# Attention scores in float32 high and low parts: from six matmuls over 64 rows to four over 128 rows

## The reference

```python
z = jnp.einsum("bqhd,bkhd->bhqk", qb, kb).astype(jnp.float32) * scale
strict = s_pos < t_pos
log_keep = jnp.where(strict, jax.nn.log_sigmoid(-z), 0.0)
after = lax.cumsum(log_keep, axis=3, reverse=True) - log_keep
weights = jnp.where(strict, jnp.exp(jax.nn.log_sigmoid(z) + after), 0.0)
outs.append(jnp.einsum("bhqk,bkhd->bqhd", weights.astype(v.dtype), vb))
```

## Time and profile before

| | us |
|---|---|
| median of 3 runs | 2956.75 (2955.31 to 2957.13) |
| the profiled execution's own time | 2955.53 |
| its span, first to last instruction | 2953.8 |
| PE busy | 2770.1 (94% of the span) |
| DVE busy | 1511.2 (51%) |
| ACT busy | 1077.0 (36%) |
| POOL busy | 985.1 (33%) |
| mean granted TensorE clock | 0.967 of full speed |
| attention stage, first score matmul to the last product | 1573.64 to about 2543 |

### The profile page before, as it was taken

One profiled execution on the slowest core, in us unless ns is written; L12 is line 12 of the kernel. 1 busy time (PEld: TensorE's weight loads), 2 busy tenths in 40 slices (PEclk: granted clock), 3 DMA queues, 4 the chain that ended last, 5 costly groups with the idle time before them and its releaser, 6 DMA issues. The chain is left out here.

```text
span 2953.8 us, 40091 instructions
## 1 busy us (share of the span) xinstructions
PE 2770.1 (94%) x14914; PEld 2031.1 (69%) x14914; DVE 1511.2 (51%) x1689; ACT 1077.0 (36%) x1590; POOL 985.1 (33%) x694
## 2 busy tenths in 40 slices
PE   4999999999999989979997999999999999689998
PEld 3999999888888857756664555555555555368887
DVE  6112445210000010008996888888889888565554
ACT  4010101111111131101114778777778777432221
POOL 1211121121211200007775655656566556200000
PEclk6999999999999999989997999999999999889999
DMA  3232221323212211114444122121221210342331
GB/s 117 85 116 99 79 71 64 114 107 118 74 64 71 78 58 67 45 45 120 129 128 140 58 58 73 37 87 51 58 87 35 82 30 26 117 137 87 98 99 43
DMA packets 165312, 239.96 MB, mean 81 GB/s; under 512 B 11152, under 2 KB 117904, under 8 KB 157504
## 3 DMA queue, kind: packets, MB, share of 16 engines
q1 hardware_dynamic: 163456, 238.25, 25.2%
q10 hardware_dynamic: 1728, 0.03, 0.0%
HBM read 141.49 MB, written 96.76 MB: 81 GB/s over the span
## 5 line engine op out<-in xcount | busy, mean ns | idle before, releaser
L1399 POOL TENSOR_TENSOR a_w<-a_beta,a_rest 128x1024 f32<-128x1024 f32 (+2 forms) x320 | 560.3, 1751 | 341.3 <-DVE a_rest L1351 311.8
L352 PE MATMUL f_acc<-ut_hi,f_w_hi 128*128 128x512 f32 (+2 forms) x1568 | 582.4, 371 | 14.6 <-POOL f_w_lo L337 14.6
L352 PE MATMUL f_acc<-ut_lo,f_w_hi 128*128 128x512 f32 (+2 forms) x1568 | 584.6, 373 | 0.0
L352 PE MATMUL f_acc<-ut_hi,f_w_lo 128*128 128x512 f32 (+2 forms) x1568 | 583.2, 372 | 0.0
L1351 DVE TENSOR_TENSOR_SCAN a_rest<-a_keep,a_rest,a_ones 128x513 f32<-128x513 f32 x384 | 466.8, 1262 | 11.0 <-ACT a_keep L1321 11.0
L1270 PE MATMUL a_turn<-a_ident,a_w 128*128 128x128 f32 (+1 forms) x2432 | 352.7, 280 | 28.1 <-DVE a_wt L1304 26.0
L1270 PEld LDWEIGHTS a_turn<-a_ident,a_w 128*128 128x128 f32 (+1 forms) x2432 | 257.4, 140 | 123.1 <-issue 64.9
L334 POOL TENSOR_TENSOR f_w_hi<-f_stage,f_zero 128x1024 fp32r<-128x1024 f32 x44 | 83.3, 1893 | 770.7 <-DMA f_stage<-in_w_blocks 770.7
L1285 PE MATMUL a_o<-a_wt,a_v 128*64 128x512 f32 (+3 forms) x1408 | 338.5, 559 | 0.0
L352 PEld LDWEIGHTS f_acc<-ut_hi,f_w_hi 128*128 128x128 f32 x1568 | 295.1, 188 | 51.0 <-issue 15.3
L352 PEld LDWEIGHTS f_acc<-ut_lo,f_w_hi 128*128 128x128 f32 x1568 | 295.0, 188 | 34.7
(11 more groups left out here) (172 smaller groups left out, 3415.8 us busy)
## 6 DMA issues: line engine op xcount, KB each, us to landing
f_stage<-in_w_blocks SPq DMA_DIRECT2D x44, 512.0 KB, 5.5
scratch_gate<-f_row_a SPq DMA_DIRECT2D x16, 1024.0 KB, 4.6
o_g<-scratch_mixed SPq DMA_DIRECT2D x32, 512.0 KB, 5.4
scratch_xbc<-f_row_a SPq DMA_DIRECT2D x12, 1032.0 KB, 4.8
s_xc<-scratch_xbc SPq DMA_DIRECT2D x16, 768.0 KB, 5.3
scratch_k_hi<-f_row_a SPq DMA_DIRECT2D x8, 1032.0 KB, 3.9
scratch_k_lo<-f_row_b SPq DMA_DIRECT2D x8, 1032.0 KB, 6.9
n_xin<-in_x SPq DMA_DIRECT2D x16, 512.0 KB, 3.5
```

The costliest lines, as they stand in the source:

```text
L352: last = nc.tensor.matmul(acc[c][:, 0:tn], w[s][:, k, :], u[:, k, t0:t0 + tn], start=(k == 0 and u is ut_hi and w is w_hi), stop=(k == KB ...
L1399: nc.gpsimd.tensor_tensor(w[r % AS][:, :, 0:tn], beta[r % KEEPS][:, :, 0:tn], rest[r % RS][:, :, 1:tn + 1], ALU.mult).then_inc(w_ready, 1)
```

## The change

The queries of a unit are no longer two tiles but one, `q`, whose rows 0 to 63 hold the high part and rows 64 to 127 the low part of one head, the head being a second dimension. The keys' high and low tiles get the same second dimension, with a head's 64 channels written twice, on rows 0 to 63 and again on rows 64 to 127. One matmul over 128 rows then gives q high times k plus q low times k; with k high and k low that is two matmuls for a head, four for a unit, each over the full array height. The product of the two low parts, which was left out before, is now in the sum. The mask matmul of a head follows its two products. Who copies what (`on_act`) is as before.

```diff
-        k_high, k_low = ring("k_high", 2, (P, T), F32R), ring("k_low", 2, (P, T), F32R)
+        k_high, k_low = ring("k_high", 2, (P, 2, T), F32R), ring("k_low", 2, (P, 2, T), F32R)
-        q_high, q_low = ring("q_high", 2, (P, W), F32R), ring("q_low", 2, (P, W), F32R)
+        q = ring("q", 2, (P, 2, W), F32R)
...
                 for tile, name in ((k_high, "k_hi"), (k_low, "k_lo")):
-                    sp.dma_start(tile[slot][:, t0:t1].bitcast(F32),
-                                 scratch[name][pair, :, t0:t1]).then_inc(k_loaded[slot][part], 16)
+                    for half in range(2):
+                        sp.dma_start(tile[slot][half * HEAD:(half + 1) * HEAD, :, t0:t1].bitcast(F32),
+                                     scratch[name][pair, :, t0:t1].rearrange("(h p) t -> p h t", h=2)
+                                     ).then_inc(k_loaded[slot][part], 16)
...
-                for tile, name in ((q_high, "q_hi"), (q_low, "q_lo")):
-                    sp.dma_start(tile[r][:, :].bitcast(F32),
-                                 scratch[name][pair, :, c * W:(c + 1) * W]).then_inc(q_loaded[r], 16)
+                for half, name in enumerate(("q_hi", "q_lo")):
+                    sp.dma_start(q[r][half * HEAD:(half + 1) * HEAD, :, :].bitcast(F32),
+                                 scratch[name][pair, :, c * W:(c + 1) * W]
+                                 .rearrange("(h p) t -> p h t", h=2)).then_inc(q_loaded[r], 16)
...
-                        pe.wait_ge(k_loaded[slot][c], START + 32 * (pair // 2 + 1))
+                        pe.wait_ge(k_loaded[slot][c], START + 64 * (pair // 2 + 1))
...
-                products = ((q_high, k_high), (q_low, k_high), (q_high, k_low))
-                for i, (q_part, k_part) in enumerate(products):
-                    for h in range(2):
-                        rows = slice(h * HEAD, (h + 1) * HEAD)
-                        mm = nc.tensor.matmul(z[n % 2][:, h, 0:tn], q_part[ch % 2][rows, qb * P:(qb + 1) * P],
-                                              k_part[slot][rows, t0:t0 + tn], start=(i == 0),
-                                              stop=(i == len(products) - 1), skip_group_check=True)
-                if diagonal(n):
-                    for h in range(2):
+                for h in range(2):
+                    for k_part in (k_high, k_low):
+                        mm = nc.tensor.matmul(z[n % 2][:, h, 0:tn], q[ch % 2][:, h, qb * P:(qb + 1) * P],
+                                              k_part[slot][:, h, t0:t0 + tn], start=(k_part is k_high),
+                                              stop=(k_part is k_low), skip_group_check=True)
+                    if diagonal(n):
```

## The result

| | before | after |
|---|---|---|
| median of 4 runs, us | 2956.94 (2955.31 to 2958.08) | 2999.31 (2998.02 to 3003.78) |
| ratio, 95% interval | | 1.0146 (1.0129 to 1.0164) |
| span of the profiled execution | 2953.8 | 3002.1 |
| PE, DVE, ACT busy | 94%, 51%, 36% | 93%, 50%, 36% |

The change costs 42.4 us. The forecast was 2993.5 us, with a range of 2974 to 3007, so it was 5.8 us too low and inside the range. The profiled execution of after is the slowest of its four, and it reaches the attention stage 3.4 us later than the one of before (first load issued at 1569.88 instead of 1566.50), in stages that the change does not touch. So the stage is compared from its own first load.

The account below looks back on a forecast made before the run. PE was taken as the bound over a pair of heads, though DVE sets the end in three stretches. 2955.5 us profiled, plus 19 for the scores and 19 for the stage's start, gave 2993.5 us, range 2974 to 3007.

Parts of the forecast that it names:

- Scores: Attention score products on PE: a fourth pass and extra weight loads add 2.4 us a pair net, 19 us over eight pairs.
- Gross: Time added to PE's score units before any hiding: 13.4 + 5.8 + 11.5, in all 30.7 us at full clock.
- Hidden: Added score time taken out of PE's waiting in three stretches where DVE is full: 1.45 us a pair.
- The turn of the array's shape: Going from 64-row scores back to 128-row transposes costs 0.10 and 0.04 us a unit, which the change removes.
- The start: Start of the attention stage, where nothing covers the loads: doubled keys on 64 partitions a transfer cost +19 us.
- half rate: Loads onto 64 partitions at the stage's start move at 209 GB/s, at 3.3 GB/s a partition.
- two bounds: Load rate at the stage's start: about 400 GB/s, costing +5.3 us, or 209 GB/s, costing +16 ahead of chunk 1.
- the queries of chunk 2: Landing near 1626 behind pair 1's keys, with their scores due at 1620: 3 us or more added to the start.
- Hidden loads: In the other seven pairs, keys load a whole pair ahead and queries some five units ahead: nothing to pay.
- Rival 1: Loads run at the old rate, so the start costs 5.3 us and the total is 2980; chance 0.30.
- Rival 2: DVE's waits hide none of the added score time: 31 + 19 gives 3005; chance 0.12.
- Rivals 3 and 4: Third: product-to-transpose price stays, 3022, chance 0.05. Fourth: turn ahead of scores goes too, 2948 or 2935, chance 0.03.

Follow-up runs that it names:

- experiment 6: Kernel before, with DVE's scan of the second head cut to 128 columns, the rest left out: 2910.99 us, ratio 0.9847.
- experiment 7: Kernel before with the new four-product scores, loads as before, and DVE's scan of the second head cut to 128 columns: 2945.71 us, ratio 0.9965.
- experiment 1: Kernel before with the new four-product scores over 128 rows, but the old loads: 2976.24 us, ratio 1.0064.
- experiment 3: Changed kernel with the same doubled key bytes and number of transfers, each over all 128 partitions; queries alike: 2979.86 us, ratio 1.0079.
- experiment 8: The changed kernel run again as it is, in another set: 2999.35 us, ratio 1.0148.
- experiment 2: Changed kernel with the old six-product scores over 64 rows, keeping the new loads (doubled keys, 64 partitions a transfer): 2981.95 us, ratio 1.0077.
- experiment 5: Changed kernel with both mask products of a diagonal unit behind its four score products: 2992.80 us, ratio 1.0122.

## Why the prediction held, point by point

**Scores.** The net size held: +2.4 us a pair forecast, +2.48 in the trace, 19 against 18.3 us. That it came out so close is partly luck, for both terms behind it were some 4 us too small and made up for each other. Gross I had 30.7; experiments 6 and 7 show 34.7. The unmasked units are 1.03 rather than 1.02 long. The masked 512-column unit costs +0.22 (1.23 less 1.01) instead of +0.18, because the second head's first step is longer than I had it. Of the narrow units, all guessed at +0.09, those of 16 and 144 columns cost +0.06 and +0.05 and those of 272 and 400 cost +0.11 and +0.17, by the medians of their times from first product to transposes: together near what I had. Hidden I had 11.6; it is about 16. I counted only what is added inside DVE's full stretches. But at a step where PE waits for DVE's copy, what was added since its last wait is taken out, up to the length of the wait: in the fourth pair, at the wait for unit 15's copy, experiment 1 adds 0.27 us less than experiment 7 does, which is the whole wait there (2.98 us less 2.71 in experiment 6), while the scores in that step itself add only 0.07.

**The turn of the array's shape.** Right: with the 64-row products gone, the step to the transposes fell from 0.32 to 0.23, and the eight transposes from 1.02 to 0.96. Without that the fourth pass would have cost 0.23 and not 0.08 in each of the 192 unmasked units. The Trainium skill, TensorEngine Tiling (Array Packing), Key Properties, says that a change of tiling mode drains the engine; the rows agree in so far as the change has a price, 0.09 and 0.06 us, but they can't show a drain. The Trainium skill, TensorE: Matmul & The Clock Gate, Part 3, has the rule that a weight load overlaps only with matmuls on another group of rows; the 0.23 steps of the changed scores speak against it, as the earlier trace rows did.

**The start.** I took the half rate out of two bounds, between which no row of before could decide, and it is right: 215 GB/s against 209 worked out, and experiment 3 separates it from the bytes. The first 16 us of it, to chunk 1, came as said (33.2 less 16.9 behind the first load is 16.3). The term that was mis-sized is the last one, the queries of chunk 2: 3 us forecast, 9.7 in the profile of after and 9.2 in that of experiment 8. With it the start cost 24 us by experiment 2, outside the 14 to 22 that I gave it. The fault was in my own sum: I let the queries land near 1626 and the scores be due at 1620, which is 6, and put down "3 or more". The rest is in the two times. Measured from the first load of before, SP issued the queries at 1620.8, near the 1621 forecast, but they took until 1628.2, and the scores were due at about 1618.5. The difference of two times that are each off by 2 us is uncertain by more than the 3 I took. The traces add up: 16.3 later at chunk 1, 1.5 gained in the units up to chunk 2 (18.8 us where before took 20.2), 9.7 of wait, in all some 24.6 later at chunk 2. Behind the wait PE ran at the lower clock for some 6 us (below).

**Hidden loads.** Right: later pairs have the same length with doubled keys (experiment 2), though the large transfers of keys (768 KB) take 11.2 and 17.5 us to land there, where they took 7.6 and 9.2.

**Sum and rivals.** The runs have 18.3 + 24.0 for my 19 + 19, so the forecast was low by the start. Rival 1, the old rate, is out by 215 GB/s; experiment 3, which makes it true, is 20 us faster, and the trace of before could not rule it out. Rival 2 named the right gross, but DVE's waits did hide half. Rivals 3 and 4 are out by the steps of 0.23 and of 0.34.

## What to carry to other kernels

Two half-height matmuls that run side by side do in three passes what stacking does in four, so stacking pays only if the shape changes that it removes are worth more than a pass; here they were not. Look at what the stacking does to the loads too: filling half the partitions halved the rate, which was free where transfers are a pair ahead and cost 20 us at the stage's start. When you estimate what a waiting engine hides of added work, count all that is added ahead of each wait and not only what is added at it. And before making the busiest engine's work shorter, ask for whom it stands still: here the ten copies, out of DVE's 33 a pair, that PE is seen to wait for were worth 37 us, twice what the changed scores cost.

## What the runs showed of the hardware beyond that

Behind a wait of 9.7 us in mid-stage PE's clock was at its lower level, 1.2 GHz, and it stayed there for some 6 us of work. Stretches of after, clock in the third column from the end:

```profile
1618.00:1622.00 4.00, 3.88 (x26) 2.40 (x24) 4.00 (x5) 3.94 (x7) 3.32 (x2) 1.00 1.01 203
1622.00:1626.00 4.00, 0.00 (x0) 0.00 (x0) 4.00 (x5) 1.54 (x2) 2.57 (x2) 0.78 1.09 248
1626.00:1630.00 4.00, 0.00 (x0) 0.00 (x0) 0.39 (x1) 0.00 (x0) 2.22 (x2) 0.50 0.97 268
1634.00:1638.00 4.00, 4.00 (x15) 1.82 (x14) 1.40 (x3) 1.11 (x3) 0.92 (x2) 0.52 0.00 0
1638.00:1642.00 4.00, 4.00 (x26) 1.99 (x24) 1.89 (x3) 2.35 (x6) 1.06 (x1) 1.00 0.00 0
```

PE was busy up to 1622, idle until 1631.61, and got the full clock back only near 1638. In between the same eight transposes took 1.85 us, from their start to that of the next row, instead of 0.96 to 1.00:

```profile
1632.81 1.92 PE L1270 MATMUL a_turn<-a_ident,a_w 128*128 128x128 f32 x8
1634.66 1.98 PE L1285 MATMUL a_o<-a_wt,a_v 128*64 128x512 f32 x4
```

The same happened at this place behind shorter waits, of 7.12 us in experiment 2 and 6.57 in experiment 5: the clock read 0.50 in the stretch of 4 us in which the work began again.
